# A hybrid attention layer on one core: a scale moved ahead of a low part, two copies moved, and seven tiles spread anew

## The reference

```
s_c = q . k_c  -> softmax over 63 compressed blocks      (o_cmp)
s_s = q . k_s  -> softmax over the selected blocks       (o_slc)
s_w = q . k_w  -> softmax over the last 512 keys         (o_win)
o_nsa = (g0 * o_cmp + g1 * o_slc + g2 * o_win) * silu(nsa_z)
o_conv = cv_b * conv3(cv_c * cv_h) * silu(cv_z)
out = x + concat(o_nsa, o_conv) @ w_out
```

## Time and profile before

| | us |
|---|---|
| median of three runs | 645.34 |
| lowest and highest | 644.18, 646.08 |
| the profiled execution, its own time | 644.26 |
| its span in the trace | 642.5 |
| TensorE busy | 630.7 |
| TensorE weight loads | 529.9 |
| VectorE busy | 486.9 |
| ScalarE busy | 381.9 |
| GpSimd busy | 206.4 |

### The profile page before, as it was taken

One profiled execution on the slowest core, in us unless ns is written; L12 is line 12 of the kernel. 1 busy time (PEld: TensorE's weight loads), 2 busy tenths in 40 slices (PEclk: granted clock), 3 DMA queues, 4 the chain that ended last, 5 costly groups with the idle time before them and its releaser, 6 DMA issues.

```text
span 642.5 us, 10218 instructions
## 1 busy us (share of the span) xinstructions
PE 630.7 (98%) x3449; PEld 529.9 (82%) x3449; DVE 486.9 (76%) x1165; ACT 381.9 (59%) x888; POOL 206.4 (32%) x220
## 2 busy tenths in 40 slices
PE   9999999999999999999999999999999999999997
PEld 6889998888888888888877888887878888787875
DVE  4955979987746754876788868898987778888853
ACT  6754457665354454555666656778776666665651
POOL 3443304343433332433224222358732221312210
PEclk9999999999999999999999999999999999999999
DMA  8523111202111111101111010133311011011101
GB/s 308 173 58 117 33 34 48 57 29 82 35 49 34 50 34 33 51 17 36 32 34 34 17 34 17 39 109 103 127 35 67 34 36 64 34 33 52 48 34 65
DMA packets 20211, 37.33 MB, mean 58 GB/s; under 512 B 2880, under 2 KB 4288, under 8 KB 20160
## 3 DMA queue, kind: packets, MB, share of 16 engines
q1 hardware_dynamic: 20016, 36.68, 18.3%
q10 hardware_dynamic: 144, 0.00, 0.0%
HBM read 32.48 MB, written 4.19 MB: 57 GB/s over the span
## 4 chain that ended last, share of the span: by engine, by line
PE 81%; DVE 13%; ACT 3%; issue 3%; POOL 0%; ACTq 0%; DVEq 0%
PE pf L1493 10%; PE pf L1494 9%; PE pf L1495 9%; PE tp L1807 5%; PE sc L1647 4%; PE pj L1493 4%; PE sc L1646 4%; PE pj L1494 4%; PE pj L1495 4%; PE po L1785 4%; PE po L1786 4%; PE sc L1493 4%; PE sc L1494 3%; PE sc L1495 3%; DVE sc L1386 2%
## 5 line engine op out<-in xcount | busy, mean ns | idle before, releaser
L1386 DVE CUSTOM_DVE_ANT_0 sc<-sc,maskb 128x64 f32<-128x64 f32 (+8 forms) x192 | 103.1, 561 | 40.1 <-PE sc L1647 39.1
L973 ACT CAST pth<-tp 128x512 fp32r<-128x512 f32 x132 | 77.6, 588 | 75.6 <-PE tp L1807 75.1
L1414 DVE TENSOR_TENSOR ptl<-tp,pth 128x512 fp32r<-128x512 f32 x132 | 90.9, 689 | 22.3 <-ACT pth L973 21.8
L691 POOL TENSOR_SCALAR qp<-qp,precip,gate 128x64 f32<-128x64 f32 x64 | 43.5, 679 | 180.2 <-DVE precip L1376 180.1
L649 POOL TENSOR_TENSOR fl<-fraw,fh 128x512 fp32r<-128x512 f32 x40 | 54.5, 1362 | 92.8 <-ACT fh L811 92.8
L1493 PE MATMUL pf<-hh,fh 128*128 128x512 f32 x200 | 80.2, 401 | 0.0
L1494 PE MATMUL pf<-hl,fh 128*128 128x512 f32 x200 | 78.3, 392 | 0.0
L1495 PE MATMUL pf<-hh,fl 128*128 128x512 f32 x200 | 78.2, 391 | 0.0
L640 POOL TENSOR_TENSOR wl<-qp,wh 128x512 fp32r<-128x512 f32 (+1 forms) x33 | 49.4, 1520 | 86.4 <-ACT wh L731 82.2
L1807 PEld LDWEIGHTS tp<-idr,qpr 128*128 128x128 f32 x560 | 62.5, 140 | 12.2 <-issue 2.6
L1807 PE MATMUL tp<-idr,qpr 128*128 128x128 f32 x560 | 65.7, 238 | 1.4 <-issue 0.7
(11 more groups left out here) (258 smaller groups left out, 1568.7 us busy)
## 6 DMA issues: line engine op xcount, KB each, us to landing
fraw<-in_wside SPq DMA_DIRECT2D x40, 256.0 KB, 2.6
qp<-in_wpack SPq DMA_DIRECT2D x28, 256.0 KB, 3.2
xo<-in_x SPq DMA_DIRECT2D x16, 256.0 KB, 2.7
out<-xo SPq DMA_DIRECT2D x16, 256.0 KB, 2.0
wor<-in_wout SPq DMA_DIRECT2D x12, 256.0 KB, 2.8
mixc<-in_xcm SPq DMA_DIRECT2D x4, 512.0 KB, 7.0
xlow<-in_xcm SPq DMA_DIRECT2D x3, 512.0 KB, 6.2
qp<-in_wpack SPq DMA_DIRECT2D x5, 224.0 KB, 2.6
```

The costliest lines, as they stand in the source:

```text
L973: nc.scalar.copy(pth[ptn % 2][:, :], tp[tpn % 2][:, :]).then_inc(pth_ready, 1)
L1386: return V.tensor_tensor_reduce(row, row, mask, -1.0, -NEG, ALU.add, ALU.min, most)
L1414: V.tensor_tensor(ptl[ptn % 2][:, :], tp[tpn % 2][:, :], pth[ptn % 2][:, :].bitcast(F32), ALU.subtract).then_inc(tp_read, 1)
```

## The change

Three edits. `turns_at` gives seven tiles the spread 2, 2, 1, 2 in place of 1, 2, 2, 2; only the selection jobs of token tile 6 have seven tiles (steps 101 to 104 and 109 to 112). The copies of the first output operand go from the steps 83 and 85 to 85 and 86. In steps with k a multiple of 4, `scale(k - 1)` stands ahead of the first tile's low part in place of behind it and the output sum.

```diff
     t = job_tiles(n)
-    return n, t[len(t) * h // 4:len(t) * (h + 1) // 4]
+    ends = (0, 2, 4, 5, 7) if len(t) == 7 else [len(t) * q // 4 for q in range(5)]
+    return n, t[ends[h]:ends[h + 1]]
...
 def mixc_half_at(k):
     for m in range(NT):
-        if step_of(OUT_0 + 16 * m - (5 if m else 9)) == k:
+        if step_of(OUT_0 + 16 * m - 5) == k:
...
 def mixn_half_at(k):
     for m in range(LAST):
-        if step_of(OUT_0 + 16 * m - (0 if m else 3)) == k:
+        if step_of(OUT_0 + 16 * m - (0 if m else 1)) == k:
...
                 _, turned = turns_at(k)
+                if 1 <= k <= NS and k % 4 == 0:
+                    scale(k - 1)
                 for kind, _ in turned[:1]:
                     prob_lo(kind)
                 u = output_at(k)
...
-                if 1 <= k <= NS and k % 4 == 0:
-                    scale(k - 1)
                 for f in side_ends(k, 0):
```

## The result

The changed kernel takes 651.73 us (median of five, 651.26 to 652.46), the kernel before 645.27 on the same chip (644.18 to 646.08). The ratio is 1.0105, with a 95% interval of 1.0093 to 1.0116: 6.0 to 7.5 us slower. The forecast was 650.9.

The account below looks back on a forecast made before the run. TensorE, busy 98% of the span, was taken as the bound, waiting for VectorE's low part. Terms summed to +5.6 us on the profiled 644.26, giving 649.8 and a median of 650.9; range 647.3 to 653.5.

Parts of the forecast that it names:

- Part 1, the cost: Scale ahead of the low part: in 17 two-tile steps from 60 on the first product comes late; ten lasting terms, 4.83 us.
- The push: Time by which the scale moved ahead sets back the first tile's low part on VectorE: 0.65 to 0.92 us by columns.
- the slack: First product's start less the end of its low part less 0.05 us; 0 to 0.54 us in the 17 steps.
- Part 1, the gain: Transposes waiting for the scaled row at the heads of steps 49, 53 and 57: −0.4 us, all put on step 57.
- Part 2: Moved copies of the first output operand, with the moved scale: +0.45 us in steps 84 to 86, +0.6 in 86 to 89.
- Part 3: Seven-tile spread: stalls of 102, 103 and 111 go; with the moved scale +0.26 us by step 104, −0.16 by step 112.
- The term of step 80: First product 0.69 us late behind the moved scale, 0.36 taken back by step 81's stall: +0.3 us.
- the 5.6 of the sum: Whole kernel: 4.83 − 0.4 + 0.45 + 0.6 + 0.26 − 0.16 = +5.6 us on the profiled execution's 644.26.
- Rival (b): Forecast plus moved scales colliding with POOL's subtractions, up to 0.4 us each: +6.8 us, median 652.1; chance 0.13.
- Its own sign: For the POOL collisions: the scale's multiplications in steps 80 and 84 take over 1 us.
- The waits on L1414: TensorE's waits on VectorE's low part in the profile after: to grow from 8.4 us to about 15.
- the 17 delays: First-product delays in the two-tile steps 60, 68 and 72 to 128 by 4: about 10 us with nothing given back.

Follow-up runs that it names:

- e5: Kernel before with the scale ahead of the low part in steps 60, 72, 108 and 116 alone: ratio 1.0047, +3.26 us in the trace.
- e6: Kernel before with the scale ahead of the low part in steps 68, 100 and 124 alone: ratio 0.9999 (0.9990 to 1.0008).
- e1: Kernel before with only the scale moved ahead of the low part, copies and spread as before: ratio 1.0096, +5.82 us in the trace.
- e2: Kernel before with only the two operand copies moved to steps 85 and 86: ratio 1.0007, +0.63 us in the trace.
- e3: Kernel before with only the seven tiles spread 2, 2, 1, 2: ratio 0.9985, −0.74 us in the trace.

## Why the prediction was right

**Part 1, the cost.** The push (0.65 to 0.92) less the slack, step by step, held to 0.07 us in the steps 60, 72, 76, 96, 108, 116, 120 and 128. e5 shows that delays last, and e6 that they are given back at a stall on a low part that doesn't move. In the steps 93 and 94 more was given back than forecast (0.58 for 0.4). Sum by the forecast, with part 1 alone: about 5.8; measured 5.8 in e1's trace.

**Part 1, the gain.** The −0.4 came as −0.3, and mostly in another place. It was put on step 57; there it is 0.07, as the multiplication and GpSimd's scaling are held by the subtraction. The head of step 57, which was to have no wait, still has one of 0.29. The rest came in steps 49 (0.13) and 50 to 55, which were priced at nothing. The head of step 53 is 1.1 ahead after the edit, and 0.8 of that is lost by step 55 to VectorE's row without a gap, as the forecast said of it.

**Part 2.** +0.45 and +0.6 came as 0.46 and 0.47 in the changed kernel. In e1, where no copy moved, the steps 84 to 86 cost 0.42 too: the 0.25 that the copies were to give in step 84 is gone by step 86, as in e2, so the first of the two sizes came out in part by luck. The second is the copy's: in the steps 87 to 90 e1 has −0.05 and e2 +0.5. Timeline of steps 86 and 87 in it, the `mixn` copy in ScalarE's row:

```profile
457.88 0.59 ACT L863 CAST qh<-tp 128x512 fp32r<-128x512 f32 x1
...
458.37 0.62 ACT L1020 CAST msh<-mixn 128x512 fp32r<-128x512 f32 x1
...
458.89 0.32 ACT L957 ACTIVATE qp<-sc,nmax 128x64 f32<-128x64 f32 x1
...
460.58 0.69 DVE L1415 TENSOR_TENSOR ptl<-tp,pth 128x512 fp32r<-128x512 f32 x1 [0.41 <-ACT pth L974]
```

**Part 3.** The stall of step 103 is gone and that of step 104 came, 1.09 at the matmul:

```profile
519.81 0.69 DVE L1216 TENSOR_TENSOR ql<-tp,qh 128x512 fp32r<-128x512 f32 x1 [1.43 <-ACT qh L863]
...
522.29 0.41 PE L1786 MATMUL po<-ptl,val 128*64 128x512 f32 x1
...
525.03 1.28 DVE L1415 TENSOR_TENSOR ptl<-tp,pth 128x512 fp32r<-128x512 f32 x2
...
525.77 0.13 PEld L1786 LDWEIGHTS po<-ptl,val 128*64 128x64 f32 x1 [1.24 <-DVE ptl L1415]
```

**What was off.** The term of step 80: +0.3 forecast, +1.4 in the changed kernel. In e1 it is 0.3 (from step 78 to 82). 1.1 are the multiplier of step 78, an instruction that no edit touches. Without it the trace's 7.0 would be 5.9, for the 5.6 of the sum; the medians differ by 6.5. Rival (b) had the mechanism, and looked for it only at the scale: there it cost 0.2 in step 80 and the gain of step 57, less than the 1.2 given to it. Its own sign, multiplications of over 1 us in 80 and 84, didn't come: they take 0.79 and 0.88. The longest in a new place are those of the steps 40 and 56 (0.99), which have one tile, so that the product falls in the next step.

The waits on L1414 were to grow from 8.4 to 15 and grew to 25.8 by that way of counting. That was an error of reading: 8.4 is the sum of two rows that count the same waits. The product's row alone grew by 8.1 us, near the 10 us that the 17 delays were summed to.

## What to carry to other kernels

When an instruction is moved ahead of another on a busy engine, ask only what waits for the one that is pushed back: the price is the push less its consumer's slack, step by step, and a delay of the bound engine lasts unless a later wait on something unmoved takes it back. A wait that is removed is worth what the next wait on the same path leaves of it: 1.57 us of waits at the heads of three steps were worth 0.3. Compare traces by the starts of the steps, less the start of the loop: that showed 0.1 us, where five rounds of timing told 0.7 us from nothing (e3) and not 0.6 us (e2). But a trace is one execution, and it can hold a loss that the median doesn't have (e6).

## What the runs showed of the hardware

VectorE and GpSimd hold each other up by whole instructions. A multiplication of 512 columns (0.55 us) took 1.00 when GpSimd's subtraction of 1.29 was under way, and 0.58 when the same subtraction came in pieces. A VectorE operation on two tensors in SBUF (0.73) took 1.78, and in the other order GpSimd's took 1.74 for 1.3. The held instruction shows no wait ahead of it: it starts, and its duration is longer; the multiplications and the multiplier ended 0.28 to 0.55 us behind the end of the other engine's instruction. The Trainium skill, "SBUF — State Buffer", section "Who interferes with whom", has both forms (a mode with two ports, and two SBUF inputs against a GpSimd operation that reads SBUF), and says that the order of issue decides who waits. For the subtractions the traces agree. For GpSimd's scaling in step 78 the starts don't tell it: it starts 0.46 us ahead of the convolution's instruction in all traces, and in ten of 14 it ends behind it. What I had not expected is the reach: which of the two comes first can change in a step that no edit touches, and then costs 1.1 us in the trace. What decided it in e6 and not in e1 stays open, as does why e6's median doesn't show it.
